# Setup of a DiT block: modulation columns by feature block, root and scaling on ScalarE

## The reference

```python
mx = jnp.split((silu(c) @ w_mod + b_mod)[:, None, :], 6, axis=-1)
mc = jnp.split((silu(c_ctx) @ w_mod + b_mod)[None, None, :], 6, axis=-1)
xn = rms_norm(x, g) * (1 + mx[1]) + mx[0]
cn = rms_norm(ctx, g) * (1 + mc[1]) + mc[0]
xr, kx, vx, gx, qx, mrx, mnx = split(xn @ w_in)
cr, kc, vc = split(cn @ w_in[:, :3072])
```

## Time and profile before

| | us |
|---|---|
| median of 3 runs | 2159.79 |
| the profiled execution | 2160.28 |
| its span | 2158.5 |

### The profile page before, as it was taken

How to read it: one execution, slowest core, us unless ns; L and a number is a source line. 1 busy time by engine, 2 the same in 40 slices (tenths; PEclk the granted TensorE clock), 3 DMA queues, 4 the chain that set the end, 5 groups by cost and what they waited for, 6 DMA issues and landing times.

```text
span 2158.5 us, 28254 instructions
## 1 busy us (share of the span) xinstructions
PE 2081.9 (96%) x10750; PEld 1763.6 (82%) x10750; DVE 1573.5 (73%) x2780; ACT 1058.9 (49%) x1627; POOL 346.4 (16%) x234
## 2 busy tenths in 40 slices
PE   5999999999999999999998999999999999999999
PEld 1778888988888888888886788887888888888887
DVE  6688598585985967859859766668998888863433
ACT  3466665765766657666676420014444333433221
POOL 0031221221212221123023000000111111110000
PEclk9999999999999999999999999999999999999999
DMA  8421212012112120121202475362122221155552
GB/s 324 116 57 40 63 48 73 19 57 64 35 38 69 51 70 30 40 61 49 64 8 98 158 281 181 127 200 100 69 78 88 88 88 68 59 177 202 182 182 86
DMA packets 85687, 209.92 MB, mean 97 GB/s; under 512 B 24624, under 2 KB 30128, under 8 KB 85424
## 3 DMA queue, kind: packets, MB, share of 16 engines
q1 hardware_dynamic: 63360, 182.95, 24.6%
q0 software_dynamic: 5792, 20.97, 2.9%
q10 hardware_dynamic: 16400, 4.19, 0.9%
HBM read 171.39 MB, written 40.89 MB: 98 GB/s over the span
## 4 chain that ended last, share of the span: by engine, by line
PE 79%; DVE 11%; ACT 4%; issue 1%; DMA 1%; POOL 0%; SPq 0%; DVEq 0%; ACTq 0%; POOLq 0%
PE banks L47 14%; PE banks L46 14%; PE banks L45 14%; PE banks L986 4%; PE banks L857 4%; PE banks L2150 4%; PE banks L2152 4%; PE banks L2151 4%; PE banks L859 4%; PE banks L858 4%; PE banks L890 3%; DVE probT_low L1488 2%; PE banks L948 2%; DVE prob L1480 1%; PE banks L930 1%
## 5 line engine op out<-in xcount | busy, mean ns | idle before, releaser
L45 PE MATMUL banks<-qh,xnh 128*128 128x384 f32 (+1 forms) x640 | 223.1, 349 | 0.3 <-PEq L211 0.3
L857 PE MATMUL banks<-xnh,wh 128*128 128x512 f32 (+1 forms) x536 | 211.5, 395 | 4.4 <-ACT stage L1092 4.1
L47 PE MATMUL banks<-qh,xnl 128*128 128x384 f32 (+1 forms) x640 | 207.4, 324 | 0.0
L46 PE MATMUL banks<-ql,xnh 128*128 128x384 f32 (+1 forms) x640 | 207.3, 324 | 0.0
L859 PE MATMUL banks<-xnh,wl 128*128 128x512 f32 (+1 forms) x536 | 204.6, 382 | 0.0
L858 PE MATMUL banks<-xnl,wh 128*128 128x512 f32 (+1 forms) x536 | 204.4, 381 | 0.0
L1488 DVE TENSOR_TENSOR probT_low<-banks,probT_high 128x512 fp32r<-128x512 f32 (+2 forms) x256 | 138.9, 584 | 56.2 <-ACT probT_high L1160 55.1
L1160 ACT CAST probT_high<-banks 128x512 fp32r<-128x512 f32 (+2 forms) x256 | 117.1, 510 | 59.7 <-PE banks L948 50.8
L45 PE MATMUL banks<-yh,wh 128*128 128x512 f32 x372 | 145.2, 390 | 0.9 <-DVE wl L2337 0.9
L46 PE MATMUL banks<-yl,wh 128*128 128x512 f32 x372 | 145.1, 390 | 0.0
L47 PE MATMUL banks<-yh,wl 128*128 128x512 f32 x372 | 144.7, 389 | 0.0
(11 more groups left out here) (357 smaller groups left out, 5804.3 us busy)
## 6 DMA issues: line engine op xcount, KB each, us to landing
raw<-w_ff SPq DMA_DIRECT2D x33, 512.0 KB, 3.7
raw<-w_down SPq DMA_DIRECT2D x33, 512.0 KB, 4.4
raw<-w_fm SPq DMA_DIRECT2D x32, 512.0 KB, 6.7
raw<-w_qkv SPq DMA_DIRECT2D x24, 512.0 KB, 3.9
raw<-w_mix SPq DMA_DIRECT2D x24, 512.0 KB, 4.9
h_d<-conv_d SPq DMA_DIRECT2D x22, 512.0 KB, 2.6
sw_d<-h_d SPq DMA_DIRECT2D x44, 256.0 KB, 2.9
raw<-w_modT SPq DMA_DIRECT2D x16, 512.0 KB, 4.7
```

The source lines that it names most:

```text
L45: pe.matmul(out, w_hi(k), x_hi(k), start=(k == 0), stop=False)
L46: pe.matmul(out, w_hi(k), x_lo(k), start=False, stop=False)
L47: last = pe.matmul(out, w_lo(k), x_hi(k), start=False, stop=(k == chunks - 1))
L857: pe.matmul(out, fh[:, s, k, :], xnh[:, k, c0:c1], start=(k == 0), stop=False)
```

## The change

Only `setup_block` and the layout of the modulation weights change. The weights come as 12 blocks of 128 output features, each [128, 8 x 128] with all eight input chunks: scale and shift blocks in turns for chunks 0 to 3 (`BLOCK_OF`), scale blocks alone for 4 to 7. `columns(n)` holds each 128 x 128 piece and streams the 2 columns of `sv`, so that the sums land as columns in PSUM; the copy of `mrow` and the 12 transposes go. The ring has 6 places of 512 KB for 4 of 768 KB. The two first weight tiles are loaded right after blocks 0 and 1; `sr` comes after block 5. The last chunk's square and sum are made in two halves. The root is ScalarE's square root, with a table load issued ahead (`warm`), and VectorE's reciprocal, and the refinement stays. The spread root is copied to SBUF by ScalarE. VectorE multiplies all eight chunks by it, ScalarE scales and shifts them (two instructions for a chunk) and rounds them, and VectorE makes the low parts; `gm` and `mod` are made chunk by chunk as their blocks come. The order of TensorE is now: block 0, sums, spread, blocks 1 to 5, units of chunk 0, blocks 6 and 7, then units of chunks 1 to 4 with one block behind each, then units of chunks 5 to 7. In the excerpt, removed lines that stand in the listing above are mostly left out.

```diff
 SEGS = ((0, C), (C, C + HALF), (C + HALF, N))
-MOD_COLS = 1536
-MOD_RING = 4
+BLOCKS = 12
+MOD_RING = 6
 ROW_BLOCKS = 4
-SCALED_EARLY = 4
-COLUMNS_EARLY = 2
...
+BLOCK_OF = {0: (0, 1), 1: (2, 3), 2: (4, 5), 3: (6, 7), 4: (8,), 5: (9,), 6: (10,), 7: (11,)}
...
-        wm = sbuf(st, "wm", [P, MOD_RING, MOD_COLS])
+        wm = sbuf(st, "wm", [P, MOD_RING, KC, P])
...
-        mt = ga[:, 0:24].rearrange("p (n w) -> p n w", w=2)
         ss = gf[:, 0:TB]
-        rs = lower[:, 0:N]
+        rs_ps, rs = lower[:, 0:N], sq[:, 0, :]
+        mt = lambda k: ga[:, 0:4] if k == 0 else lower[:, HALF * ((k - 1) % 3):HALF * ((k - 1) % 3) + 4]
+        PIECES = (slice(0, N // 2), slice(N // 2, N))
+        SIDES = ((slice(0, C), 1), (slice(C, N), 0))
...
+                def load_block(n):
+                    if n >= MOD_RING:
+                        sp.wait_ge(wm_used, n - MOD_RING + 1)
+                    sp.dma_start(wm[:, n % MOD_RING, :, :].rearrange("p k c -> p (k c)"), w_modb[n])\
+                      .then_inc(wm_in[n % MOD_RING], 16)
...
-                load_wm(0)
+                load_block(0)
+                load_block(1)
+                for n in range(2):
+                    sp.dma_start(raw[:, n, :], w_fm[0, :, 1024 * n:1024 * n + 1024]).then_inc(raw_in[n], 16)
+                for n in range(2, 6):
+                    load_block(n)
                 sp.dma_start(sr[:, :, :], bass.AP(tensor=c_rows.tensor, offset=0, ap=[[0, P], [D, 2], [1, D]]))\
                   .then_inc(sr_in, 16)
-                load_wm(1)
                 load_rows(0)
-                load_wm(2)
+                load_block(6)
                 load_rows(1)
-                load_wm(3)
-                sp.dma_start(raw[:, 0, :], w_fm[0, :, 0:1024]).then_inc(raw_in[0], 16)
-                load_wm(4)
-                sp.dma_start(raw[:, 1, :], w_fm[0, :, 1024:2048]).then_inc(raw_in[1], 16)
-                load_wm(5)
+                for n in range(7, 10):
+                    load_block(n)
                 load_rows(2)
-                load_wm(6)
+                load_block(10)
                 load_rows(3)
-                load_wm(7)
+                load_block(11)
                 sp.dma_start(raw[:, 2, :], w_qkv[0, :, 2048:3072]).then_inc(raw_in[2], 16)
                 for s in range(2):
                     sp.wait_ge(w_lo, s + 1)
...
-                pool.memset(power[:, :], -0.5).then_inc(memset_done, 1)
-                pool.wait_ge(memset_done, 3)
-                pool.wait_ge(mean_square, 1)
-                pool.tensor_tensor(rms[:, 1, :], rms[:, 0, :], power[:, :].broadcast_to([P, TB]), ALU.pow)\
-                    .then_inc(root_done, 1)
+                pool.wait_ge(memset_done, 2)
...
+                def columns(n):
+
+                    k = [c for c in BLOCK_OF if n in BLOCK_OF[c]][0]
+                    part = BLOCK_OF[k].index(n)
+                    pe.wait_ge(wm_in[n % MOD_RING], (n // MOD_RING + 1) * 16)
+                    if k >= 1:
+                        pe.wait_ge(rs_copied, 1)
+                    if k >= 4:
+                        pe.wait_ge(gm_done, 2 * k - 4)
+                    for c in range(KC):
+                        last = pe.matmul(mt(k)[:, 2 * part:2 * part + 2], wm[:, n % MOD_RING, c, :], sv[:, c, :],
+                                         start=(c == 0), stop=(c == KC - 1))
                     last.then_inc(wm_used, 1)
...
+                def first_units(k):
+                    pe.wait_ge(w_lo, 2)
                     pe.wait_ge(lo_done, k + 1)
...
+
+                columns(0)
+                for half in range(2):
+                    pe.wait_ge(summed, KC - 1 + half)
+                    for b in range(TB // 2 * half, TB // 2 * half + TB // 2):
+                        last = pe.matmul(ss[:, b:b + 1], total[:, P * b:P * b + P], ones[:, 0:1], start=True, stop=True)
+                last.then_inc(mean_done, 1)
+                pe.wait_ge(rstd_done, 1)
+                for b in range(TB):
+                    last = pe.transpose(rs_ps[:, P * b:P * b + P], rms[:, 1, b:b + 1].broadcast_to([P, P]), ident[:, :])
+                last.then_inc(spread, 1)
+                for n in range(1, 6):
+                    columns(n)
+                first_units(0)
+                columns(6)
+                columns(7)
+                for k in range(1, 5):
+                    first_units(k)
+                    columns(7 + k)
+                for k in range(5, KC):
+                    first_units(k)
...
-                    act.activation(sq[:, k % 2, :], xs[:, k, :], ACT.Square).then_inc(squared, 1)
-                act.wait_ge(sr_in, 16)
-                act.activation(sr[:, :, :], sr[:, :, :], ACT.Silu).then_inc(sr_done, 1)
+                    for cols in PIECES if k == KC - 1 else (slice(0, N),):
+                        act.activation(sq[:, k % 2, cols], xs[:, k, cols], ACT.Square).then_inc(squared, 1)
+                act.wait_ge(memset_done, 2)
+                act.activation(warm[:, :], eps[:, :], ACT.Sqrt)
+                act.wait_ge(mean_square, 1)
+                act.activation(rms[:, 2, :], rms[:, 0, :], ACT.Sqrt).then_inc(root_done, 1)
                 for s in range(2):
                     act.wait_ge(raw_in[s], 16)
                     act.copy(flat(wh, s), raw[:, s, :]).then_inc(w_hi, 1)
-
-                act.wait_ge(wm_used, KC)
-                act.copy(mrow[0:2, :, :], acc[0:2, 0:3, :]).then_inc(mod_copied, 1)
+                act.wait_ge(spread, 1)
+                act.copy(rs, rs_ps).then_inc(rs_copied, 1)
                 for k in range(KC):
-                    act.wait_ge(scaled, k + 1)
-                    if k < SCALED_EARLY:
-                        act.copy(xnh[:, k, :], xs[:, k, :]).then_inc(hi_done, 1)
-                    else:
-                        act.activation(xnh[:, k, 0:C], xs[:, k, 0:C], ACT.Identity, bias=mod[:, k, 1:2])
-                        act.activation(xnh[:, k, C:N], xs[:, k, C:N], ACT.Identity, bias=mod[:, k, 0:1])\
-                           .then_inc(hi_done, 1)
+                    act.wait_ge(normed, k + 1)
+                    act.wait_ge(gm_done, 2 * k + 2)
+                    for cols, w in SIDES:
+                        act.activation(xs[:, k, cols], xs[:, k, cols], ACT.Identity, bias=mod[:, k, w:w + 1],
+                                       scale=gm[:, w, k:k + 1]).then_inc(scaled, 1)
+                    act.wait_ge(scaled, 2 * k + 2)
+                    act.copy(xnh[:, k, :], xs[:, k, :]).then_inc(hi_done, 1)
+                    if k == 1:
+                        act.wait_ge(sr_in, 16)
+                        act.activation(sr[:, :, :], sr[:, :, :], ACT.Silu).then_inc(sr_done, 1)
+                act.wait_ge(wm_used, BLOCKS)
                 for j in range(3):
                     act.wait_ge(raw_in[j], 16 if j == 2 else 32)
                     act.copy(q_part(qh, j), raw[:, j, :]).then_inc(w_hi, 1)
...
                 def normalize(k):
-                    then(dve.tensor_tensor(xs[:, k, :], xs[:, k, :], rs, ALU.mult))
-
+                    dve.wait_ge(rs_copied, 1)
+                    dve.tensor_tensor(xs[:, k, :], xs[:, k, :], rs, ALU.mult).then_inc(normed, 1)
+
+                def columns(k):
+
+                    dve.wait_ge(wm_used, BLOCK_OF[k][-1] + 1)
+                    shift = mt(k)[:, 2:4] if k < 4 else dots[:, k - 4, :]
+                    dve.tensor_scalar(mod[:, k, :], shift, bm[:, k:k + 1], None, ALU.add).then_inc(gm_done, 1)
+                    dve.tensor_scalar(gm[:, :, k], mt(k)[:, 0:2], bm1[:, k:k + 1], gain[:, 0, k:k + 1],
+                                      ALU.add, ALU.mult).then_inc(gm_done, 1)
+
+                def token_low(k):
+                    dve.wait_ge(hi_done, k + 1)
+                    dve.tensor_tensor(xnl[:, k, :], xs[:, k, :], xnh[:, k, :].bitcast(F32), ALU.subtract)\
+                       .then_inc(lo_done, 1)
...
+                then(dve.tensor_scalar(bm1[:, :], bm[:, KC:2 * KC], 1.0, None, ALU.add))
...
+                    for n, cols in enumerate(PIECES if k == KC - 1 else (slice(0, N),)):
+                        dve.wait_ge(squared, k + 1 + n)
+                        if k >= 2 and n == 0:
+                            dve.wait_ge(summed, k - 1)
+                        dve.tensor_tensor(total[:, cols], total[:, cols], sq[:, k % 2, cols], ALU.add).then_inc(summed, 1)
                 dve.wait_ge(mean_done, 1)
                 dve.tensor_scalar(rms[:, 0, :], ss, 1.0 / D, EPS, ALU.mult, ALU.add).then_inc(mean_square, 1)
-                shift_dots(0)
                 dve.wait_ge(root_done, 1)
                 v, r, w = (rms[:, n, :] for n in range(3))
+                then(dve.reciprocal(r, w))
                 then(dve.tensor_tensor(w, v, r, ALU.mult))
                 then(dve.scalar_tensor_tensor(w, w, -0.5, r, ALU.mult, ALU.mult))
                 dve.scalar_tensor_tensor(r, w, 1.5, r, ALU.add, ALU.mult).then_inc(rstd_done, 1)
+                split_low(0)
```

(89 more changed lines are left out.)

7 lines of the change are left out of this document (1 added, 6 removed).

## The result

The changed kernel takes 2169.34 us (median of 7 runs, 2165.04 to 2170.33) beside 2161.64 us for the kernel before (7 runs); the ratio is 1.0037, 95% interval 1.0028 to 1.0047. It is slower by 8 us. The profiled execution took 2170.10 us with a span of 2167.9, beside 2160.28 and 2158.5.

What follows compares the result with a forecast made beforehand. TensorE, last to end setup, bounds it: chunk 0 starts at 49.9, plus 26.7 for eight chunks, 11.2 for blocks 6 to 11 and 1.9 for a clock fall: 89.7, 5.6 later, so 2166 us; range 2151.8 to 2170.

Steps and rivals of the forecast that it cites:

- The bound: Setup stage: TensorE is last to end it, at 84.07 us, so the change is worth what it moves that end.
- The clock: TensorE before `first_units(0)`: narrow work for some 20 to 30 us does not raise the granted clock from 0.50.
- the sum: TensorE's setup times added up: setup ends at 89.7 us, 5.6 later than 84.07.
- The pitch: Modulation blocks on TensorE at the low clock level: 0.216 us per weight load with its matmul, 3.4 us a block.
- Loads don't slow at the low level: Rival for the modulation blocks: 0.116 us per load and matmul throughout, setup 5.7 us sooner, 2154.6 us; chance 0.07.
- The root: Setup, after the sums: POOL's power, 2.88 us, goes; the chain takes 1.5 us instead of 4.0.
- the spread: Setup, TensorE's 10 transposes after the root: up to doubled from 1.31 to 2.2 us, ending at 32.9.
- the scaling: Setup, per chunk: ScalarE 2.9 us and 0.3 of waits, VectorE 3.4, both hidden behind TensorE's 5.0 up to chunk 4.
- SP's queue: Weight loads in setup: blocks 10, 11 wait behind late rows, yet block 10 lands some 9 us before TensorE wants it.
- the second fall: Clock drop after blocks 6 and 7 in setup: comes about every second time, put in at 1.9 us.
- the low start of chunk 0: First chunk of `first_units` starts at the low clock level: 4.96 us instead of 3.11, 1.85 more.

## Why the prediction was right

*The bound.* TensorE ended setup in every version, and the time followed its end: setup ends at 84.07, 91.35, 78.18 and 74.31 against medians of 2161.6, 2169.3, 2156.0 and 2151.7.

*The clock.* The step that carried the sum, that narrow work does not bring the high level, held: blocks 1 to 5 with two columns take 16.9 us in all four versions that have them, and streaming 128 columns in all blocks instead is worth 13 us. That it doesn't was my estimate from the earlier trace rows, where the level fell in 128-column transposes behind a pause; no run tests transposes by themselves. Being busy did not bring it: TensorE worked without a gap from 32.92 to 49.85, and the pace stayed at 0.213 us a pair.

*The pitch.* 0.216 was taken, 0.213 measured; first units were put at 49.9 and came at 49.85. "Loads don't slow at the low level" falls with it. The loads themselves take 187 to 192 ns at the high level and 333 at the low, and a pair takes 0.106 to 0.116 us at the high level and 0.213 at the low.

*The root, the spread, the scaling, SP's queue.* POOL's power, 2.88 us, is gone, and the chain took 1.3 us against 1.5. The table load for the square root took 1.28 us, from 21.55 to 22.83, beside VectorE's last sums, which end at 23.01, and ScalarE was then idle for 6.56 us before the root at 29.61. The silu of `sr` took 1.28 us for its table load from 46.75 and 1.91 for itself, 3.2 together as taken. The rest: the spread's end at 32.9 as summed; VectorE and ScalarE idle for TensorE; no wait for a block's load after the first. Chunk 0, though, was ready at 45.0 us and not by 41.5: its low part stands behind chunk 1's columns in VectorE's order and waits for block 3. That cost nothing, since TensorE came to it at 49.85.

*The term that was mis-sized* is the second fall, and beside it the low start of chunk 0. I put 1.9 us for a fall that comes every second time. In the profiled execution it came and made chunk 1 take 5.9 us instead of 3.1, 2.8 more. Chunk 0 took 5.7 us, 0.7 more than the 4.96 that I carried over from before. Together they are the step from 87.8, the sum without a second fall, to 91.35, while two other executions without the second fall ended at 87.04 and 87.95. Whether it comes more often than every second time isn't shown: six of the change's seven runs lie at 2168 and above, but the version whose blocks 6 to 11 stream 128 columns scatters just as much. These 1.7 us over the forecast's 89.7 and the 2.1 us behind setup are 3.8 of the 4.2 us between the profiled 2170.1 and the forecast of 2166. The later stretches were in no term of mine, and that they came out on the slow side is luck of the execution. The median of 2169.34 is 7.7 us above that of the kernel before, where I said 5.6.

## What to carry to other kernels

Before turning a matmul so that the small operand streams, ask what TensorE's clock will do: here 17 us with 2 or 32 streamed columns per weight load ran at 0.213 us a pair for 0.109, busy throughout, and the loads slowed from 187 to 333 ns with it. Streaming padding up to 128 columns was free here (a block of 16 pairs takes 1.70 us at the high level with 2 columns and with 128) and was worth more than the rewrite. And a chain that is shortened while a longer one runs beside it (here the root in the order of before, the halves of the last sum) gives nothing: look at what releases the next user.

## What the runs showed that was not expected

128 streamed columns per load, most of them zeros, brought the level; 32 did not. A pair costs the same with both at the high level: 0.109 us with 128 columns in blocks 6 and 7, 0.109 with 2 in the run with the last chunk in one piece. The level rose early in block 1 there, though 3.5 us of the same work in block 0 some 10 us earlier had not brought it. And setup ended 4 us apart in two executions whose instructions are the same from chunk 0 on (91.35 and 87.04): in one the level fell in the narrow work of blocks 6 and 7, in the other it did not.
